# Routing tables in bf16, expert weights split earlier, and a separate buffer for the second gate weights in a two-layer encoder with a mixture of experts

## The reference

```python
s = sigmoid(t @ w_router)                     # t: 544 rows x 1024
sel = s + b_router
grp = argmax(sum of the two best sel of each of the 4 groups)
idx = the two best of sel inside the group     # first one on ties
w = s[idx] / sum(s[idx])
gates = sum over k of one_hot(idx[k]) * w[k]
a = silu(t @ w_gate[e]) * (t @ w_up[e])        # 1024 -> 512, every expert e
a = a * gates
x = x + g2 * (sum over e of a @ w_down[e])     # 512 -> 1024
```

## Time and profile before

| what | us |
|---|---|
| median of 3 runs (1583.99 to 1591.72) | 1584.24 |
| time of the profiled execution | 1588.31 |
| its span in the trace | 1586.5 |
| PE matmul busy in the span | 1385.3 (87%) |
| DVE busy | 1028.7 (65%) |
| ACT busy | 869.6 (55%) |
| POOL busy | 188.9 (12%) |

### The profile page before, as it was taken

How to read it: one execution, slowest core, us unless ns; L and a number is a source line. 1 busy time by engine, 2 the same in 40 slices (tenths; PEclk the granted TensorE clock), 3 DMA queues, 4 the chain that set the end, 5 groups by cost and what they waited for, 6 DMA issues and landing times.

```text
span 1586.5 us, 27602 instructions
## 1 busy us (share of the span) xinstructions
PE 1385.3 (87%) x10165; PEld 1135.9 (72%) x10165; DVE 1028.7 (65%) x1547; ACT 869.6 (55%) x1545; POOL 188.9 (12%) x260
## 2 busy tenths in 40 slices
PE   4799999989749999999929999999794599999990
PEld 2688887757537888888819888887473488888870
DVE  1756543236467999989876444443565488989986
ACT  3334355453317888888733444443512278888872
POOL 1111111110001212222000000000000012222210
PEclk8799999989859999999969999999797699999995
DMA  8465633242418999999953633343505389999984
GB/s 311 126 201 190 220 116 115 75 174 81 159 62 298 368 372 370 388 378 382 377 184 82 187 123 115 115 128 114 185 18 215 108 312 371 370 368 373 386 312 187
DMA packets 167821, 357.58 MB, mean 225 GB/s; under 512 B 20770, under 2 KB 82978, under 8 KB 159026
## 3 DMA queue, kind: packets, MB, share of 16 engines
q1 hardware_dynamic: 155380, 331.94, 58.7%
q0 software_dynamic: 12352, 24.40, 4.3%
HBM read 340.56 MB, written 33.54 MB: 236 GB/s over the span
## 4 chain that ended last, share of the span: by engine, by line
PE 82%; DVE 7%; issue 3%; DMA 3%; ACT 3%; SPq 1%; DVEq 1%; ACTq 0%; POOL 0%; POOLq 0%
PE bank L609 20%; PE bank L611 19%; PE bank L610 19%; PE bank L320 3%; PE bank L2403 2%; PE bank L1588 2%; PE bank L1550 2%; PE bank L695 2%; PE bank L762 1%; PE bank L1565 1%; DMA ring<-in_w_ada 1%; PE bank L1015 1%; PE bank L2431 1%; PE bank L1554 1%; PE bank L945 1%
## 5 line engine op out<-in xcount | busy, mean ns | idle before, releaser
L610 PE MATMUL bank<-ring_r,arena_r 128*128 128x512 f32 x816 | 321.4, 394 | 0.0
L609 PE MATMUL bank<-ring_r,hT_r 128*128 128x384 f32 x512 | 185.3, 362 | 0.0
L2111 DVE TENSOR_TENSOR ring_r<-ring,arena_r 128x1024 fp32r<-128x1024 f32 x128 | 150.9, 1222 | 43.8 <-ACT arena_r L2104 43.3
L610 PEld LDWEIGHTS bank<-ring_r,arena_r 128*128 128x128 f32 x816 | 155.6, 191 | 30.7
L611 PE MATMUL bank<-ring_r,work_r 128*128 128x384 f32 x512 | 172.8, 337 | 0.0
L610 PE MATMUL bank<-ring_r,hT_r 128*128 128x384 f32 x512 | 172.2, 336 | 0.0
L2111 DVE TENSOR_TENSOR ring_r<-ring,hT_r 128x1024 fp32r<-128x1024 f32 x144 | 169.5, 1217 | 2.7 <-ACT hT_r L2104 1.5
L2104 ACT ACTIVATE hT_r<-ring 128x1024 fp32r<-128x1024 f32 x144 | 149.8, 1056 | 35.8 <-DMA ring<-in_w_gate 32.6
L2111 DVE TENSOR_TENSOR ring_r<-ring,work_r 128x1024 fp32r<-128x1024 f32 x136 | 160.3, 1219 | 14.0 <-ACT work_r L2104 13.6
L2104 ACT ACTIVATE arena_r<-ring 128x1024 fp32r<-128x1024 f32 x128 | 128.4, 1053 | 52.0 <-DMA ring<-in_w_down 52.0
L2104 ACT ACTIVATE work_r<-ring 128x1024 fp32r<-128x1024 f32 x136 | 137.2, 1060 | 3.0 <-DMA ring<-in_w_up 3.0
(11 more groups left out here) (356 smaller groups left out, 2634.6 us busy)
## 6 DMA issues: line engine op xcount, KB each, us to landing
ring<-in_w_gate SPq DMA_DIRECT2D x136, 512.0 KB, 7.0
ring<-in_w_up SPq DMA_DIRECT2D x136, 512.0 KB, 7.5
ring<-in_w_down SPq DMA_DIRECT2D x68, 1024.0 KB, 9.2
bc<-in_w_ada SPq DMA_DIRECT2D x40, 1024.0 KB, 7.9
bc<-in_w_in_even SPq DMA_DIRECT2D x64, 192.0 KB, 5.6
bc<-in_w_in_odd SPq DMA_DIRECT2D x64, 192.0 KB, 3.6
arena<-moe_out SPq DMA_DIRECT2D x8, 1024.0 KB
ring<-in_w_ada SPq DMA_DIRECT2D x3, 2048.0 KB, 13.8
```

The source lines that it names most:

```text
L609: nc.tensor.matmul(acc, rows_hi, w_hi, start=first, stop=False)
L610: nc.tensor.matmul(acc, rows_hi, w_lo, start=False, stop=False)
L2111: dve.tensor_tensor(r32(piece(m_low[v], q)), piece(m_low[v], q), f32(piece(m_high[v], q)), ALU.subtract).then_inc(MO[f"lo_{c}"], 1)
```

## The change

It has these parts.

1. **Earlier high parts.** SP loads u first, then g, stores the rows, and loads d last. ACT makes u 0 and 1 high in `out_act` ahead of its last `evacuate`, g 0 and 1 at the start of `route_act` ahead of its wait for the router logits, g 2 and 3 behind the exponentials; then it loads the activation table of silu, which was the first thing of `moe_act`.
2. **Low parts moved.** DVE makes u 0 and 1 low at the start of `route_dve`, g 0 while PE inverts the table, and g 1 to 3 behind the barrier, at the start of `moe_dve`.
3. **Shorter routing chain.** Three PSUM copies and a memset of DVE go; the add reads PSUM itself.
4. **bf16 tables.** `slot_hot`, `item_hot` and `item_val` become bf16. The row number is split into a tile offset and a row within the tile; PE multiplies these in ten bf16 products. The gates are split by POOL into three bf16 parts (four small operations and three multiplies of 250 numbers), PE multiplies them in ten more products into `bank[3]`, and DVE adds the three sums into `slot_gate` as its last step ahead of the barrier.
5. **Gather.** POOL gathers the first rows straight by `slot_tok[:, 0:1]`, behind its gate work and without the copy.
6. **Second gate weights.** The g slab of the second item goes to a buffer of its own in `bc`, loaded right behind the barrier; ACT makes all its four pieces high ahead of its wait for the first up product, and DVE all four low ahead of the first product.
7. **Order in the loop.** DVE: g piece 0 low, `rows_low`, `product`, g pieces 1 to 3 low (before: `product`, g 0 and 1, `rows_low`, g 2 and 3).
8. **End of the loop.** The last results go to a buffer of their own, `m_y_last`, and don't wait for the scatter before.

The core of the diff:

```diff
+            split_high(act, "u", layer_first(act, l), 0, 1)
             evacuate(TILES - 1)
...
-        slot_hot = rt2[:, 0:1280].rearrange("p (n s) -> p n s", s=P)
-        item_ge = rt2[:, 1280:1540].rearrange("p (n i) -> p n i", i=MAX_ITEMS + 1)
-        item_hot = rt2[:, 1540:1790].rearrange("p (n i) -> p n i", i=MAX_ITEMS)
-        item_val = rt2[:, 1790:2290].rearrange("p (n i) -> p n i", i=2 * MAX_ITEMS)
...
+        slot_hot = rt_b[:, 0:1280].rearrange("p (n s) -> p n s", s=P)
+        item_hot = rt_b[:, 1280:1530].rearrange("p (n i) -> p n i", i=MAX_ITEMS)
+        item_val = rt_b[:, 1536:1536 + 50 * MAX_ITEMS].rearrange("p (n i) -> p n i", i=5 * MAX_ITEMS)
...
+            pe.wait_ge(s["split"], 7 * (l + 1))
+            for ct in range(2 * TILES):
+                r = rows(ct % TILES)
+                last = nc.tensor.matmul(bank[3][:, 0:3 * MAX_ITEMS], slot_hot[0:r, ct, :], item_val[0:r, ct, 2 * MAX_ITEMS:],
+                                        start=ct == 0, stop=ct == 2 * TILES - 1)
+            last.then_inc(s["map"], 1)
...
+            split_high(act, "g", first, 0, 1)
             act.wait_ge(s["turned"], l + 1)
...
-            split_high(act, "g", first, 0, 1, 2, 3)
-            split_high(act, "u", first, 0, 1)
+            split_high(act, "g", first, 2, 3)
+            act.preload_act_table(ACT.Silu)
...
+            lk = Link(pool, s["split"], base=7 * l)
+            flat = gates[:, :, :].rearrange("p c t -> p (c t)")
+            pool.wait_ge(s["near"], l + 1)
+            lk.do(pool.tensor_copy(gate_part[0], flat))
+            lk.do(pool.tensor_tensor(gate_rest, flat, gate_part[0], ALU.subtract))
+            lk.do(pool.tensor_copy(gate_part[1], gate_rest))
+            lk.do(pool.tensor_tensor(gate_part[2], gate_rest, gate_part[1], ALU.subtract))
+            for k in range(3):
+                lk.step(pool.tensor_tensor(item_val[:, :, (2 + k) * MAX_ITEMS:(3 + k) * MAX_ITEMS], item_hot,
+                                           gate_part[k].unsqueeze(2).to_broadcast([P, 2 * TILES, MAX_ITEMS]), ALU.mult))
             pool.wait_ge(s["h"], 32 * (l + 1))
             pool.wait_ge(s["slots"], l + 1)
-            item_rows_in(pool, layer_first(pool, l), 0)
+            first_rows_in(pool)
...
+            split_low(dve, "u", first, 0, 1)
             dve.wait_ge(s["cnt"], l + 1)
...
-            lk.do(dve.tensor_copy(cnt, bank[1][:, TILES * NE:(TILES + 1) * NE]))
...
-            lk.do(dve.tensor_copy(dst[:, 0:NT * NE], bank[1][:, 0:NT * NE]))
-            lk.do(dve.memset(dst[:, NT * NE:TILES * NE], 0.0))
-            lk.do(dve.tensor_copy(dst[0:DEC, NT * NE:TILES * NE], bank[1][0:DEC, NT * NE:TILES * NE]))
-            lk.do(dve.tensor_tensor(T3(dst, NE), T3(dst, NE), bt(st, NE), ALU.add))
+            lk.step(dve.tensor_tensor(T3(dst[:, 0:NT * NE], NE), T3(bank[1][:, 0:NT * NE], NE),
+                                      st.unsqueeze(1).to_broadcast([P, NT, NE]), ALU.add))
+            lk.do(dve.tensor_tensor(dst[0:DEC, NT * NE:TILES * NE], bank[1][0:DEC, NT * NE:TILES * NE], st[0:DEC, :], ALU.add))
...
-            lk.step(dve.tensor_tensor(item_val[:, :, 0:MAX_ITEMS], item_hot, wide(row_no, MAX_ITEMS), ALU.mult))
-            lk.do(dve.tensor_tensor(item_val[:, :, MAX_ITEMS:2 * MAX_ITEMS], item_hot,
-                                    wide(gates[:, :, :].rearrange("p c t -> p (c t)"), MAX_ITEMS), ALU.mult))
+            lk.step(dve.tensor_scalar(item_val[:, :, MAX_ITEMS:2 * MAX_ITEMS], item_hot, row_in, None, ALU.mult))
+            lk.do(dve.tensor_tensor(item_val[:, :, 0:MAX_ITEMS], item_hot, wide(tile_no, MAX_ITEMS), ALU.mult))
...
+            split_low(dve, "g", first, 0)
+            dve.wait_ge(s["map"], 2 * l + 1)
             lk.do(dve.tensor_scalar(row_of, bank[2][:, 0:MAX_ITEMS], -1.0, None, ALU.add))
+            lk.do(dve.tensor_tensor(row_of, bank[2][:, MAX_ITEMS:2 * MAX_ITEMS], row_of, ALU.add))
...
+            dve.wait_ge(s["map"], 2 * l + 2)
+            lk.do(dve.tensor_copy(slot_gate[:, :], bank[3][:, 2 * MAX_ITEMS:3 * MAX_ITEMS]))
+            lk.do(dve.tensor_tensor(slot_gate[:, :], bank[3][:, MAX_ITEMS:2 * MAX_ITEMS], slot_gate[:, :], ALU.add))
+            lk.do(dve.tensor_tensor(slot_gate[:, :], bank[3][:, 0:MAX_ITEMS], slot_gate[:, :], ALU.add))
             rt_self[0] += lk.n
-            first = layer_first(dve, l)
-            split_low(dve, "g", first, 0, 1, 2, 3)
-            split_low(dve, "u", first, 0, 1)
             phase_end("dve", dve)
...
-            for c in "gud":
-                load(c, 0)
+            load("u", 0)
+            load("g", 0)
...
+            load("d", 0)
             sp.wait_ge(g["phase"], PH[f"route{l}"])
...
-                sp.wait_ge(s["g"], n + 1)
-                load("g", e)
+                if down:
+                    sp.wait_ge(s["g"], n + 1)
+                    load("g", e)
+                else:
+                    load("g", e, raw=second_gate)
...
-                split("g", n + 1, 0, 1)
+                    split("g", n + 1, 0, 1)
+                else:
+                    split("g", n + 1, 0, 1, 2, 3, raw=second_gate)
                 act.wait_ge(s["u"], n + 1)
                 rows_high(n + 1)
-                split("g", n + 1, 2, 3)
                 if before:
+                    split("g", n + 1, 2, 3)
                     results_before(n, stored)
...
-            results_before(last + 1, last, bank[2:4])
+            results_before(last + 1, None, bank[2:4], m_y_last)
...
+            split("g", first, 1, 2, 3)
...
-                product(n)
-                split("g", n + 1, 0, 1)
-                rows_low(n + 1)
-                split("g", n + 1, 2, 3)
+                    split("g", n + 1, 0)
+                    rows_low(n + 1)
+                    product(n)
+                    split("g", n + 1, 1, 2, 3)
+                else:
+                    split("g", n + 1, 0, 1, 2, 3, raw=second_gate)
+                    product(n)
+                    rows_low(n + 1)
                 split("u", n + 1, 0, 1)
 
```

More of the change, by code:

```diff
@@ L586, in lead_pe @@
             fuse_product(pe, l, NT, 0, KD)
-        RT = sems("rt", "logits", "part", "e", "turned", "self", "mask", "pos", "cnt", "near", "far", "map", "slots", "h")
+        RT = sems("rt", "logits", "part", "e", "turned", "self", "mask", "pos", "cnt", "near", "far", "map", "split", "slots", "h")
         def logit_bank(j):
@@ L2103, in split_high, with split_low @@
                         act.wait_ge(MO[f"wd{q // 2}"], 16 * n)
-                act.activation(r32(piece(m_high[v], q)), piece(m_low[v], q), ACT.Copy).then_inc(MO[f"hi_{c}"], 1)
-        def split_low(dve, c, n, *pieces, last_down=False):
+                act.activation(r32(piece(m_high[v], q)), piece(m_low[v] if raw is None else raw, q), ACT.Copy).then_inc(MO[f"hi_{c}"], 1)
+        def split_low(dve, c, n, *pieces, last_down=False, raw=None):
             v = slab_of(c, last_down)
```

53 lines of the change are left out of this document (34 added, 19 removed).

## The result

The changed kernel takes 1558.87 us (median of 4 runs, 1558.40 to 1563.73) where the kernel before takes 1585.91 us beside it: a ratio of 0.9829, 95% interval 0.980 to 0.9858. The forecast was 1555 us, in a range of 1544 to 1568, and faster. The changed kernel was timed twice more, on two other occasions: 0.983 (0.9811 to 0.985) and 0.9831 (0.9809 to 0.9853). The sum of the prediction was 29.4 us; the three comparisons give 27.0, 25.8 and 25.4.

The account below looks back on a forecast made before the run. PE was taken as the bound (82% of the chain), with gains only in its gaps outside the balanced loop; 16.2 + 7.2 + 1 + 5 = 29.4 us off 1584.24 gave 1554.8, said as 1555, range 1544 to 1568.

Parts of the forecast that it names:

- Earlier high parts: Ahead of and in routing: early u and g copies hidden in idle time, 0 us; 0.4 us charged in layer 1.
- Chain and map: Routing stage: DVE's shorter chain saves 0.7 us, the bf16 map 3.9 us; slots known at 449.6 instead of 453.31.
- Barrier and first product: Routing's end to first gate product: 458.95 instead of 467.25, 8.3 us; both layers 16.6 less 0.4.
- barrier at 453.0: End of layer 0's routing stage: barrier after PE's second ten products and three adds, before at 462.85.
- The rule on GpSimd: POOL's gate work: GpSimd contends with VectorE instructions having two SBUF inputs; with it in full, barrier 1 us later.
- the second lockout: POOL's gate work in routing: held up by DVE's g 0 remainder as well as L2300, beginning at 448.3, ending at 451.3.
- Second item: Passage from first to second item: 2.1 us sooner and 1.5 us of clock per layer, together 7.2 us.
- Loop order: DVE's new order in the item loop: 1 us gained in all, bounds +4.8 and -4.
- Tails: Ends of the two loops: last results start behind PE, gaining 4.0 and 1.0 us; 2 instead of 4 if scatter held.
- the smaller gain (1565): Rival, chance 0.15: POOL lockout, no clock gain, first scatter and late gather take 10 us from the start-up gain.
- The loop did not turn slower: Rival, chance 0.04: `product` at the up product's end comes late, some 30 blocks each pay 1.2 us; 1592 us.
- the gaps did not close: Rival, chance 0.12: all PE gaps in the loop close, 4.8 us instead of 1, POOL never in the way; 1549 us.

Follow-up runs that it names:

- the second profile: The changed kernel run again with no edit: 1561.17 us, ratio 0.983 to the kernel before.
- the experiment with the rows behind one piece: Changed kernel with VectorE taking the first rows' remainders behind one gate piece instead of three after the barrier: 1559.69 us, ratio 0.9821 to the kernel before.

## Why the prediction was right

**Earlier high parts: 0.** Right in layer 0. ACT had 1.24 us left ahead of its eviction, and DVE's chain started 0.07 us sooner against the stretch before it. In layer 1 DVE's two u remainders end a little too late, 0.7 us instead of the 0.4 charged.

**Chain and map.** Right. From the first step behind the exponentials to the first `slot_hot` DVE takes 13.30 us (434.84 to 448.14) where it took 14.19: 0.9 for the 0.7 of the shorter chain. The slots are known at 449.5 in the positions of the prediction (2.80 us taken off those of the trace), which had 449.6.

**Barrier and first product: 16.6 less 0.4, measured 13.2.** This is the term that was mis-sized; in layer 0 it was 8.3 and measured 7.0. The steps inside it, in the same positions: POOL's multiplies end at 450.8, predicted 451.3; the gather starts at 451.0, predicted 451.8; DVE is done at 452.9, predicted 452.9; the barrier is at 454.5, predicted 453.0. That one step failed: "barrier at 453.0" took DVE's last add as the last arrival. I had seen POOL's gather, priced its issue and even the landing of its rows at 3.3 us from the start (3.4 measured), and did not ask what POOL's `drain` behind it waits for. It ended 0.1 us behind the landing of the rows in all 18 stretches where it set the barrier. The second half of the miss is layer 1, which I took as a copy: there the rows landed 4.1 to 4.4 us behind the gather's start, and 7.9 us became 6.2 (5.7 in the second profile). Before, the same drain was hidden: the gather started at 455.04 and DVE had work until 462.79. The step from barrier to first product was right: 5.95 predicted, 5.78 measured, and the experiment with the rows behind one piece shows that it was DVE's queue, as the working says.

**The rule on GpSimd.** The first two gate operations took 0.72 and 1.06 us beside DVE's two-input instructions, and the second 0.20 without. The VectorE instructions beside them end 0.05 us ahead of them. By this the trace agrees with the Trainium skill, "GPSIMD Engine Reference", Key points. It changed the time by little: with the second lockout gone the gather came 0.3 us sooner. The prediction had it in one direction only: VectorE's small steps, of one input too, took 0.47 to 0.57 us beside POOL's two-input multiplies, and 0.18 without.

**Second item: 7.2.** Right: 2.2 us at its start in each layer, and 1.2 and 2.3 us of clock. **Loop order: 1.** The runs can't tell it from 0; the bounds held. The two terms together can be read from the loops: 331.12 / 298.50 before, 328.1 / 293.4 on average after, 8.2 us for 8.2 predicted. That they agree so well is luck, as one loop scatters by up to 5 us from execution to execution, and of the kernel before there is one profile only.

**Tails: 4.0 and 1.0.** 3.7 and 1.1 in two profiles, 2.5 and 1.1 in the first one, where the remainders of L669 held the first add. The bound that I gave, a scatter held back by the DMA engines, did not occur: the last scatter of layer 0 landed 3.3 us behind its issue, as before.

**Sum.** 13.2 + 8.2 + 4.8 = 26.2 us for 29.4 predicted, between the measured 25.4 and 27.0. The 3 us that are missing are those of the barrier in the two layers. Of the rivals none came about: the smaller gain (1565) had POOL late as one of four parts, and that part did come, at 1.5 us in layer 0 and 2.5 in layer 1 behind DVE's last step, and by the drain, not by the gates. The loop did not turn slower, and the gaps did not close.

## What to carry to other kernels

When the work that sets a barrier moves away, ask of every other engine when it arrives, its drain included: here a drain behind a gather lasted until its rows had landed, which stays unseen as long as another engine is later. Behind a barrier, look at the order of the first queue: two pieces that nobody needs yet, ahead of the one that everybody waits for, cost here as much as the drain, and as both delays end at the same step, taking away either gave the whole 1.4 us. And to move the order of two steps in a loop whose loads are late moved the gaps and not their sum, as far as one loop's scatter of 5 us lets one see.

## What the runs showed of the hardware

POOL's `drain` behind an indirect gather of 128 rows ended 0.1 us behind the landing of the rows, in 18 stretches of nine profiles in which the landing came from 3.23 to 4.35 us behind the gather's start; the gather's own row lasts 1.1 to 1.2 us. A POOL operation on 128x10 numbers takes 0.20 us alone; beside a two-input instruction of DVE it ended 0.05 us behind that instruction, after 0.72 and 1.06 us. Multiplies of 128x250 bf16 take 0.60 to 0.64 us, and 0.93 beside a two-input step of DVE; beside them DVE's steps on 128x25 numbers take 0.47 to 0.57 us and not 0.18. And in unchanged code the loop of layer 0 took from 325.97 to 331.10 us in ten profiled executions, and the stretch between the layers from 393.8 to 399.4 in thirteen: a difference of less than 5 us in them can't be read from one profile.
